# A two-block transformer kernel: eight weight tiles used twice at the end of each feed-forward stage, and the row transposes one projection tile later in the mixer

## The reference

```
for l in range(DEPTH_2):                                  # DEPTH_2 = 2
    h = 0.5 * _swiglu(x, ffn_w_gate[l, 0], ffn_w_up[l, 0], ffn_w_down[l, 0])
    x = _layernorm_2(ALPHA * x + h, ln_g[l, 0], ln_b[l, 0])
    h = _mixer(x, w_in[l], ..., w_out[l], band_bias, valid)
    x = _layernorm_2(ALPHA * x + h, ln_g[l, 1], ln_b[l, 1])
    h = 0.5 * _swiglu(x, ffn_w_gate[l, 1], ffn_w_up[l, 1], ffn_w_down[l, 1])
    x = _layernorm_2(ALPHA * x + h, ln_g[l, 2], ln_b[l, 2])

def _swiglu(x, wg, wu, wd):
    return (jax.nn.silu(x @ wg) * (x @ wu)) @ wd          # 1024 -> 2816 -> 1024
```

## Time and profile before

| | us |
|---|---|
| median of 3 runs | 2618.5 |
| lowest and highest | 2614.92, 2619.34 |
| span of the profiled execution | 2615.5 |
| PE busy in it | 2465.8 (94%) |
| DVE busy | 1412.0 (54%) |
| ACT busy | 1013.5 (39%) |

### The profile page before, as it was taken

The page is one execution under the profiler, slowest core; times in us unless marked ns, Lnnn a source line. Parts: engine busy times, 40 slices in busy tenths (PEclk is TensorE's granted clock), DMA queues, the critical chain, the costliest instruction groups (busy, mean ns, idle before and its releaser), DMA issues. The chain is left out here.

```text
span 2615.5 us, 33377 instructions
## 1 busy us (share of the span) xinstructions
PE 2465.8 (94%) x12238; PEld 2051.4 (78%) x12238; DVE 1412.0 (54%) x2055; ACT 1013.5 (39%) x1448; POOL 54.3 (2%) x84
## 2 busy tenths in 40 slices
PE   7998959999699999998999999999999988999998
PEld 4877837888588888786798888888888867988886
DVE  5887578999643332588733323533323786533324
ACT  6345347777422221246332222222222454322211
POOL 0011010000100000000000000000000000000000
PEclk9999979999899999999999999999999999999999
DMA  6764659999643332330333334323323312333332
GB/s 241 284 214 141 258 222 370 402 407 403 255 120 96 96 96 91 99 88 33 97 97 96 96 97 119 91 78 97 97 90 105 92 57 65 97 90 96 97 95 73
DMA packets 310486, 381.62 MB, mean 146 GB/s; under 512 B 14540, under 2 KB 227180, under 8 KB 310262
## 3 DMA queue, kind: packets, MB, share of 16 engines
q1 hardware_dynamic: 300744, 345.10, 39.7%
q0 software_dynamic: 6896, 26.22, 2.6%
q10 hardware_dynamic: 2750, 8.99, 0.8%
HBM read 346.17 MB, written 34.10 MB: 145 GB/s over the span
## 5 line engine op out<-in xcount | busy, mean ns | idle before, releaser
L1656 DVE TENSOR_TENSOR w_part_lo<-w_raw,w_part_hi 128x1024 fp32r<-128x1024 f32 x252 | 308.3, 1225 | 734.3 <-ACT w_part_hi L1652 733.5
L1652 ACT ACTIVATE w_part_hi<-w_raw 128x1024 fp32r<-128x1024 f32 x252 | 266.9, 1062 | 794.5 <-PE PS L1662 760.2
L1660 PE MATMUL PS<-xT_hi,w_part_hi 128*128 128x512 f32 (+1 forms) x1472 | 556.7, 378 | 14.2 <-PEq L1928 8.3
L1661 PE MATMUL PS<-xT_lo,w_part_hi 128*128 128x512 f32 (+1 forms) x1472 | 555.0, 377 | 0.0
L1662 PE MATMUL PS<-xT_hi,w_part_lo 128*128 128x512 f32 (+1 forms) x1472 | 555.0, 377 | 0.0
L1660 PEld LDWEIGHTS PS<-xT_hi,w_part_hi 128*128 128x128 f32 x1472 | 279.8, 190 | 67.8 <-DVE w_part_lo L1656 15.7
L1661 PEld LDWEIGHTS PS<-xT_lo,w_part_hi 128*128 128x128 f32 x1472 | 279.5, 190 | 50.1 <-issue 0.2
L1662 PEld LDWEIGHTS PS<-xT_hi,w_part_lo 128*128 128x128 f32 x1472 | 279.6, 190 | 49.9
L1660 PE MATMUL PS<-w_part_hi,h_hi 128*128 128x512 f32 x576 | 228.1, 396 | 0.0
L1661 PE MATMUL PS<-w_part_lo,h_hi 128*128 128x512 f32 x576 | 227.8, 395 | 0.0
L1662 PE MATMUL PS<-w_part_hi,h_lo 128*128 128x512 f32 x576 | 227.8, 395 | 0.0
(11 more groups left out here) (470 smaller groups left out, 4052.4 us busy)
## 6 DMA issues: line engine op xcount, KB each, us to landing
expert_w_raw<-in_w SPq DMA_DIRECT2D x136, 512.0 KB, 7.3
w_raw<-in_ffn_w_gate SPq DMA_DIRECT2D x88, 512.0 KB, 3.8
w_raw<-in_ffn_w_up SPq DMA_DIRECT2D x88, 512.0 KB, 3.8
w_raw<-in_ffn_w_down SPq DMA_DIRECT2D x88, 512.0 KB, 3.8
w_raw<-in_w SPq DMA_DIRECT2D x68, 512.0 KB, 6.3
w_raw<-in_w_in SPq DMA_DIRECT2D x56, 512.0 KB, 4.8
late_raw<-in_w_ada SPq DMA_DIRECT2D x32, 512.0 KB, 5.7
w_raw<-in_w_out SPq DMA_DIRECT2D x24, 512.0 KB, 4.8
```

The lines of the kernel that those rows point to most:

```text
L1652: nc.scalar.activation(t.hi, raw[t.n % 4], ACT.Copy).then_inc(w_hi, 1)
L1656: nc.vector.tensor_tensor(t.lo, raw[t.n % 4], t.hi.bitcast(f32), ALU.subtract).then_inc(w_lo, 1)
L1660: nc.tensor.matmul(out, a[0][a_at], b[0][b_at], start=first, stop=False, skip_group_check=True)
L1661: nc.tensor.matmul(out, a[0][a_at], b[1][b_at], start=False, stop=False, skip_group_check=True)
```

## The change

- The last **eight** down tiles are used twice instead of six. Four are kept in the memory of `xT` (now tiles 14 to 17), two in new buffers `tail_hi` and `tail_lo` (tiles 18 and 19), the last two (20 and 21) in the ring as before.
- In the second pass their order is `DOWN_SECOND`: the four of `xT`, then the two of the ring, then the two of the new buffers. The transposes stand after four tiles, as before, so four tiles follow them instead of two.
- `ring_free` counts after an ffn as it did after a mixer: `USED[s] - 3` and `USED[s] - 2`, the uses of the two ring tiles.
- In the mixer, unit 3 is computed and evacuated before the transposes of half 1.
- The tables of uses grow by two for each ffn.

```diff
+TAIL = 8
-FFN_TILES, FFN_USES = 66, 80
+FFN_TILES, FFN_USES = 66, 82
+DOWN_SECOND = [0, 1, 2, 3, 6, 7, 4, 5]
...
-    USED = [0, 80, 114, 194, 274, 308]
+    USED = [0, 82, 116, 198, 280, 314]
...
         if s == 0:
             return 0
-        return USED[s] - (3 if s - 1 in MIXERS else 1) + k
+        return USED[s] - 3 + k
...
-        if k < 60:
+        if k < FFN_TILES - TAIL:
             return Part(n, *ring(k), u + k + 9, u + k + (7 if k >= 10 else 1), 0, turns)
-        if k < 64:
-            at = 2 * (k - 60)
-            return Part(n, flat(xT_hi[:, at:at + 2, :]), flat(xT_lo[:, at:at + 2, :]), u + k + 15, u + 52, u + k + 9)
-        return Part(n, *ring(k), u + k + 15, u + k + 3, u + k + 9)
+        place = k - (FFN_TILES - TAIL)
+        first, used = u + k + 9, u + 52 + N_DOWN + DOWN_SECOND.index(place) + 1
+        if place < 4:
+            return Part(n, flat(xT_hi[:, 2 * place:2 * place + 2, :]), flat(xT_lo[:, 2 * place:2 * place + 2, :]), used, u + 52, first)
+        if place < 6:
+            return Part(n, tail[0][:, place - 4, :], tail[1][:, place - 4, :], used, 0, first)
+        return Part(n, *ring(k), used, u + k + 1, first)
...
+            tail_hi = sb(c, f"tail_hi{s}", [P, 2, D], f32r)
+            tail_lo = sb(c, f"tail_lo{s}", [P, 2, D], f32r)
...
-                    for n in range(N_DOWN - 6):
+                    for n in range(N_DOWN - TAIL):
                         if n == FC // 2:
                             pe.wait_ge(f["sum_done"], q0 + UNITS)
                         down(n, range(TB))
-                    for n in range(N_DOWN - 6, N_DOWN):
+                    for n in range(N_DOWN - TAIL, N_DOWN):
                         down(n, (0, 1))
-                    for n in range(N_DOWN - 6, N_DOWN):
-                        if n == N_DOWN - 2 and not final:
+                    for at, place in enumerate(DOWN_SECOND):
+                        if at == 4 and not final:
                             transposes(pe, s + 1, 0)
-                        down(n, (2, 3))
+                        down(N_DOWN - TAIL + place, (2, 3), at == TAIL - 1)
...
-                    for u in range(3):
+                    for u in range(4):
                         unit(u)
                     transposes(pe, s, 1)
-                    for u in range(3, 17):
+                    for u in range(4, 17):
                         unit(u)
...
-                    for u in range(3):
+                    for u in range(4):
                         evacuate(u)
                     for kc in range(KC):
                         turn_act(act, s, 1, kc)
-                        if kc in (3, 5, 7):
-                            evacuate({3: 3, 5: 4, 7: 5}[kc])
+                        if kc in (5, 7):
+                            evacuate({5: 4, 7: 5}[kc])
```

More of the change, by code:

```diff
@@ L1680, in ring_free, with ffn_tile @@
             return 0
-        return USED[s] - (3 if s - 1 in MIXERS else 1) + k
-    def ffn_tile(s, k, h=None, turns=0):
+        return USED[s] - 3 + k
+    def ffn_tile(s, k, h=None, tail=None, turns=0):
         n, u = FIRST[s] + k, USED[s]
@@ L1909, in ffn @@
             H = (h_hi, h_lo)
-            T = lambda k, turns=0: ffn_tile(s, k, H, turns)
+            tail_hi = sb(c, f"tail_hi{s}", [P, 2, D], f32r)
+            tail_lo = sb(c, f"tail_lo{s}", [P, 2, D], f32r)
+            T = lambda k, turns=0: ffn_tile(s, k, H, (tail_hi, tail_lo), turns)
             class Unit:
@@ L2056, in _ @@
                     if final:
-                        dve.wait_ge(w_used, T(N_FFN - 1).used)
+                        dve.wait_ge(w_used, T(N_UP + N_DOWN - TAIL + DOWN_SECOND[-1]).used)
                         ln_sums_dve(dve, 1)
@@ L2095, in _, with down @@
                             unit(Unit(8 + c2, ii))
-                    def down(n, blocks):
+                    def down(n, blocks, last_of_second=False):
                         half, kp = n // (FC // 2), n % (FC // 2)
@@ L2106, in down @@
                                 last = product(PS[:, (0 if half else 4) + b, :], H, (slice(None), kc, slice(b * P, (b + 1) * P)), (t.hi, t.lo),
-                                               (slice(None), slice(kk * HALF, (kk + 1) * HALF)), kc == 0, kc == FC - 1)
+                                               (slice(None), slice(kk * HALF, (kk + 1) * HALF)), kc == 0, kk == 1 and (last_of_second if blocks == (2, 3) else kp == FC // 2 - 1))
                         last.then_inc(w_used, 1)
-                    for n in range(N_DOWN - 6):
+                    for n in range(N_DOWN - TAIL):
                         if n == FC // 2:
```

## The result

| | before | after |
|---|---|---|
| median of 5 runs, us | 2619.34 | 2604.21 |
| lowest and highest | 2614.92, 2619.35 | 2600.91, 2609.53 |
| ratio, 95% interval | | 0.9949 (0.9937 to 0.9960) |

The change saves 0.51%, by the ratio 13.4 us (10.5 to 16.5). The medians lie 15.1 apart; I go by the ratio, which is taken over all runs. A second set of five runs of the same kernel, beside other runs of the kernel before, gave 2603.95 and a ratio of 0.9954 (0.9940 to 0.9967).

What follows compares the result with a forecast made beforehand. TensorE, busy for 94% of the 2615.5 us span, was taken as the bound. Barriers 7.0, stage 3 1.4, mixers 2.1 and 2.05 sum to 12.5 us, taking the median of 2618.5 to 2606.0 us, range 2603 to 2611.

Steps and rivals of the forecast that it cites:

- The barrier: At the three feed-forward barriers: TensorE's step shrinks from 3.13, 3.28 and 3.13 us to 0.86, gaining 7.0 us.
- The cover of 3.0 us: At the feed-forward barriers: TensorE ends 3.0 us after VectorE's last lo part, so it comes last.
- Stage 3: Feed-forward stage 3 starts at full clock behind a short pause, as stage 2 does, gaining 1.4 us.
- The mixers: At both mixers' starts: unit 4 starts 13.3 us after the barrier, gaining 2.1 and 2.05 us.
- Unit 6: In the mixers: half 1 is turned by about 17.8 us after the barrier, unit 6 starts at 19.1; cost zero.
- The gain reaches the end of the mixer: Mixer's first block: VectorE's long stretch, which ends the block, starts earlier, so the 2.1 and 2.05 us are kept.
- Eight tiles in time: Feed-forward stages: ScalarE splits the kept tiles some 10 us earlier, with over seven us of cover; cost nothing.
- a fixed 1.5 us: Behind feed-forward barriers: a pause of 2.7 to 2.9 us costs itself and about 1.5 us of half speed.
- the clock that stays low behind a short pause: Rival at the feed-forward barriers: half speed still costs 1.5 us per start; gain 8.2 us, 2610.3 us; chance 9%.
- The mixer giving the gain back: Rival in the mixers: VectorE's long stretch is anchored elsewhere, so 4.15 us is lost; 2610.1 us; chance 9%.
- The unmoved barrier: Rival at the feed-forward barriers: another engine still comes last, only the mixers' units gain; 2617.3 us; chance 7%.
- Slow turning: Rival in the turns: eight turns over 6.5 us make unit 6 wait; at 12 us the time is 2630; chance 3%.

Runs made afterwards that it cites:

- the copies: Changed kernel plus 4, 5, 6 or 8 needless VectorE copies ending each feed-forward block but the last: 2602.65, 2603.01, 2608.89, 2618.45 us.
- the first two experiments: Changed kernel with only its feed-forward part, 2608.35 us; kernel before with only the mixer part, 2614.03 us.
- the feed-forward part alone: Changed kernel with eight tiles and ring tiles before the kept ones, but unit 3 again behind the mixer's transposes: 2608.35 us, ratio 0.9966.
- the mixer part alone: Kernel before with only unit 3 moved ahead of the transposes of half 1: 2614.03 us, ratio 0.9983.
- the copies ahead of VectorE's pause: Changed kernel plus two needless VectorE copies in each mixer, before VectorE's pause of about 3 us: 2601.47 us; the same two behind it: 2606.39 us.

## Why the prediction was right, point by point

**The barrier**, 7.0 us: measured are steps of 0.71, 0.86 and 0.71 in place of 3.13, 3.28 and 3.13, 7.3 us. The forecast took the step of the mixer's barrier for all; behind stages 0 and 3 it is 0.15 shorter. The cover of 3.0 us was right to a tenth, by the copies.

**Stage 3**, 1.4: from first to last product start it takes 2034.16 - 1666.48 = 367.68, in place of 369.32, so 1.6. Stage 2 without the steps went from 367.95 to 367.70. These 0.25 are not a gain of the eight tiles: the same kernel once more has 368.11 there, and over the kernels with eight tiles stage 2 takes 367.7 in some profiles and 368.1 in others. So some 0.2 of the 1.6 is scatter of this kind. The clock gave 1.4: with the ring tiles last, where it falls behind this barrier, stage 3 takes 369.06 and stage 2 367.67.

**The mixers**, 2.1 and 2.05: unit 4 starts 13.14 and 13.15 after the barrier where 13.3 was forecast, and the first blocks are 2.23 and 2.19 shorter in this profile, 1.78 and 2.57 in the second. The two parts of the change do need each other, as the traces of the first two experiments show: at unit 4 the feed-forward part alone leaves this term at zero, and the mixer part alone brings 0.9.

**Unit 6**, no cost: turns ready 17.75 after the barrier (forecast 17.8), unit 6 at 18.98 (19.1).

**The gain reaches the end of the mixer**: yes; the 2.98 us of pause are still there in the profile after, and the copies show that VectorE's stretch behind it is what counts. One reading of this step was wrong: the first block does not end with VectorE. Before the change, too, ScalarE ends last, at 1199.04, and VectorE at 1198.63. That the sum held all the same is because VectorE's stretch holds up TensorE's last units, and these ScalarE.

**Eight tiles in time**: the three splits for `xT` in a row start at 1048.53 after, which is 1043.2 in the time of the trace before, where they start at 1054.28: 11 us earlier. The cover was larger than the prediction had it: it put the start of the first pass 14 half tiles before the transposes, but eight of the first pass and four of the second are 12, and the trace after has it at 1058.50, 33.5 us before them. The lo part of tile 21 is ready at 1066.81, 11 us before TensorE uses it, and no wait for it appears.

The sum of these, 7.3 + 1.6 + 2.2 + 2.2, is 13.3. The two profiles compared say 13.15, the ratio 13.4, the ratio of the second set 12.0, and the forecast was 12.5. That the number is so near is in part luck: the attention blocks, which the sum leaves out, scatter by 2 us and more.

**What was mis-sized is the clock.** The prediction treated the half speed behind a pause of 2.7 to 2.9 us as a fixed 1.5 us. Over the traces of the kernels that have this pause (before, mixer part alone, ring tiles last) there are nine such barriers; the clock fell behind eight, for 3 us in seven and for 6 us in one, where it moved the transposes by 2.7 us (14.14 after the barrier in place of 11.48). In five of the seven nothing else holds TensorE up before the transposes, and these come 12.8 to 13.0 after the barrier, 1.3 to 1.5 late. So the term is nothing, 1.3 to 1.5, or 2.7 us, and 1.5 is the upper end of the usual case.

Of the rivals, the clock that stays low behind a short pause is refuted by ten profiles, after and experiments, with 0.32 to 1.94 us of idle time at each of their three feed-forward barriers: the clock stayed up at all thirty. The mixer giving the gain back is refuted by the copies ahead of VectorE's pause. The unmoved barrier is what the order of tiles without ring tiles first gives. Slow turning did not come: with the stop for unit 4 the eight turns took 6.3 us from the transposes on (1116.77 to 1123.04), and unit 6 began 7.5 after them. That 7.5 is the limit from which unit 6 waits; the 6.5 of the prediction was too low by its own figures (19.1 - 11.6), and with it the 4.9 that it gives for twelve microseconds of turning should be 4.5.

## What to carry to other kernels

When a block ends with a barrier, let the last work of the bounding engine be work that holds no buffer which the others wait for: using the ring's tiles before the kept ones took out three pauses at the price of two more buffers. How much lead is left can be measured by adding needless work to the other engine until the time moves. Before counting a gain at the head of a block, look for the last pause of the engine that bounds it, which need not be the one that ends it: here it stood behind the gain, so the gain went through, and it was also room into which two more taps could move.

## What the runs showed of the hardware

The length of a pause alone does not decide what the clock of TensorE does after it, and these traces do not show what else does. At the barriers of the feed-forward stages idle times up to 1.94 us left it at 1.00 (thirty of thirty), 2.73 to 2.88 brought it to 0.50 in eight of nine cases, 3.29 to 3.45 in three of three. Elsewhere a shorter pause did it too. Two profiles of the same kernel, after, have the same wait in the first mixer, 1.80 and 1.81 us. In the first the clock stays up behind it, in the second it falls:

```profile
1171.10:1173.00 1.90, 1.90 (x8) 1.59 (x9) 1.68 (x7) 0.81 (x3) 0.00 (x0) 1.00 0.00 0
1173.00:1175.00 2.00, 2.00 (x10) 1.66 (x9) 1.76 (x4) 0.00 (x0) 0.00 (x0) 1.00 0.01 4
```

```profile
1166.50:1168.00 1.50, 1.50 (x7) 1.21 (x8) 1.29 (x7) 0.79 (x3) 0.00 (x0) 0.97 0.00 0
1168.00:1170.00 2.00, 2.00 (x6) 1.61 (x5) 1.93 (x4) 0.00 (x0) 0.00 (x0) 0.50 0.01 4
1170.00:1172.00 2.00, 2.00 (x7) 1.55 (x7) 1.76 (x4) 0.00 (x0) 0.00 (x0) 0.67 0.00 0
```

The first block of the mixer then takes 94.60 or 95.05 us. The attention blocks have pauses of 2.4 and 3.0 us at their barriers and many short ones. Behind the first block of stage 1 the mean granted clock is 0.95 over 98.0 us in the first profile and 1.00 over 95.5 us in the second, so there, too, the difference goes with the clock. It goes some way towards explaining why whole executions of one kernel scatter by several microseconds while stages 2 and 3 repeat to half of one; no run shows that it is all of it. The Trainium skill, "TensorE: Matmul & The Clock Gate", Part 1, says of the slow start that its length varies from run to run; these traces agree, and the loss behind one pause of 2.7 to 2.9 us ranged from nothing to 2.7 us.
